# Key transposes within the second projection, a third pair of split buffers, query transposes in two parts, and compression's activation last in VectorE's queue

## The reference, cut to what matters

```
h = rms_norm(x, g_mix_norm[l]);  z = h @ w_in[l]
q, kc, vc, ks_, vs_, kw_, vw_, gl, hc, cg, bg = split(z)
q = rms_norm(q per head, g_q)                                  # 8 heads of 64
k_cmp = rms_norm(compress(kc, pe[0], w1[0], b1[0], w2[0], b2[0]), g_k[0])
v_cmp = compress(vc, pe[1], w1[1], b1[1], w2[1], b2[1])
k_slc, k_win = rms_norm(ks_, g_k[1]), rms_norm(kw_, g_k[2])
attn_out = nsa_attention(q, k_cmp, v_cmp, k_slc, vs_, k_win, vw_, gates)

def compress(k_raw, pe, w1, b1, w2, b2):     # blocks of 32 tokens, stride 16: 31 of them
    blk = blocks(k_raw) + pe
    return gelu(blk @ w1 + b1) @ w2 + b2     # w1: 2048 x 256, w2: 256 x 64
```

## Time and profile before

| | us |
|---|---|
| median of 3 runs | 1664.21 (1662.63 to 1664.91) |
| the profiled execution's own time | 1665.39 |
| its span | 1663.6 |
| TensorE busy | 1528.0 |
| GpSimd busy | 586.5 |
| VectorE busy | 764.7 |
| ScalarE busy | 455.9 |

### The profile page before, as it was taken

The page is one execution under the profiler, slowest core; times in us unless marked ns, Lnnn a source line. Parts: engine busy times, 40 slices in busy tenths (PEclk is TensorE's granted clock), DMA queues, the critical chain, the costliest instruction groups (busy, mean ns, idle before and its releaser), DMA issues.

```text
span 1663.6 us, 21240 instructions
## 1 busy us (share of the span) xinstructions
PE 1528.0 (92%) x8362; PEld 1205.2 (72%) x8362; DVE 764.7 (46%) x1461; ACT 455.9 (27%) x722; POOL 586.5 (35%) x481
## 2 busy tenths in 40 slices
PE   6978999899999999989999999999999989976885
PEld 5867787778888888867888878775588866544442
DVE  2343756549687774345513730255412254423234
ACT  4233233433131322342323332343222221100001
POOL 2473121235445444434533234421144313322222
PEclk9988999999999999989999999999999999999897
DMA  5222111034544452222322112220043589999995
GB/s 228 76 90 77 38 40 38 26 126 158 216 173 176 189 202 84 94 82 100 109 76 101 51 51 102 79 83 26 2 176 148 221 331 353 377 393 373 394 412 201
DMA packets 37348, 260.92 MB, mean 157 GB/s; under 512 B 7280, under 2 KB 7920, under 8 KB 13184
## 3 DMA queue, kind: packets, MB, share of 16 engines
q1 hardware_dynamic: 31488, 251.13, 40.0%
q0 software_dynamic: 5760, 8.41, 1.6%
HBM read 252.69 MB, written 17.30 MB: 162 GB/s over the span
## 4 chain that ended last, share of the span: by engine, by line
PE 82%; DVE 8%; issue 4%; ACT 4%; POOL 2%; DMA 1%; DVEq 0%; SPq 0%; ACTq 0%; POOLq 0%
PE G L2050 13%; PE G L2051 13%; PE G L2052 12%; PE SA L2578 4%; PE G L2578 4%; PE SA L2050 3%; PE SA L2052 3%; PE SA L2051 3%; PE PB L2052 3%; PE PB L2051 3%; PE PB L2050 3%; PE OB L2234 2%; PE G L2092 1%; PE SA L2467 1%; PE PB L2586 1%
## 5 line engine op out<-in xcount | busy, mean ns | idle before, releaser
L736 POOL TENSOR_TENSOR wl<-raw,wh 128x512 fp32r<-128x512 f32 x364 | 487.4, 1370 | 694.7 <-ACT wh L869 689.9
L869 ACT ACTIVATE wh<-raw 128x2048 fp32r<-128x2048 f32 x91 | 174.1, 1913 | 296.5 <-PE SA L2052 152.5
L2050 PE MATMUL G<-Hh,wh 128*128 128x512 f32 x544 | 218.1, 401 | 4.9 <-DVE arena L1482 1.7
L2051 PE MATMUL G<-Hl,wh 128*128 128x512 f32 x544 | 214.3, 394 | 0.0
L2052 PE MATMUL G<-Hh,wl 128*128 128x512 f32 x544 | 214.1, 394 | 0.0
L1553 DVE SCALAR_TENSOR_TENSOR arena<-arena,st 128x256 f32<-128x256 f32 x144 | 132.9, 923 | 5.1
L2050 PEld LDWEIGHTS G<-Hh,wh 128*128 128x128 f32 x544 | 103.8, 191 | 26.1 <-issue 2.3
L2052 PEld LDWEIGHTS G<-Hh,wl 128*128 128x128 f32 x544 | 103.6, 190 | 22.5
L2051 PEld LDWEIGHTS G<-Hl,wh 128*128 128x128 f32 x544 | 103.9, 191 | 20.0
L809 POOL DMA_INDIRECT raw<-xn_rows,arena x38 | 36.6, 962 | 130.4 <-PE G L2594 106.1
L2050 PE MATMUL G<-wh,Hh 128*128 128x256 f32 x256 | 77.6, 303 | 0.5 <-DVE arena L1293 0.5
(11 more groups left out here) (520 smaller groups left out, 3127.2 us busy)
## 6 DMA issues: line engine op xcount, KB each, us to landing
raw<-in_pieces_dram SPq DMA_DIRECT2D x91, 1024.0 KB, 4.8
arena<-in_pieces_dram SPq DMA_DIRECT2D x24, 1024.0 KB, 4.8
arena<-in_wexp_dram SPq DMA_DIRECT2D x11, 2048.0 KB
dn_w<-in_wexp_dram SPq DMA_DIRECT2D x18, 1024.0 KB, 42.1
arena<-in_wexp_dram SPq DMA_DIRECT2D x12, 1024.0 KB, 29.2
gu_y<-in_wexp_dram SPq DMA_DIRECT2D x6, 2048.0 KB
gu_z<-in_wexp_dram SPq DMA_DIRECT2D x5, 2048.0 KB, 45.9
gu_h<-in_wexp_dram SPq DMA_DIRECT2D x4, 2048.0 KB
```

The costliest lines, as they stand in the source:

```text
L736: ins = pool.tensor_tensor(low_[:, part], whole[:, part], high[:, part], ALU.subtract)
L869: act.activation(wh[:, split_slot(s)], wait_raw(act, sp_list[s]), ACT.Copy).then_inc(S("high_split"), 1)
L2050: pe.matmul(out, ah, bh, start=first, stop=False)
L2051: pe.matmul(out, ah, bl, start=False, stop=False)
```

## The change

TensorE takes `cT` 0 and 1 after the first half of ksvs and `cT` 2 and 3 after the second; kwvw follows. VectorE's block additions now stand ahead of the key squares, and the k squares use another part of `arena`. A third pair of split buffers, `third`, lies beneath the `alibi` table and holds piece 5 alone; the slots of later pieces alternate from there. The bias tables, whose place it shares, are therefore loaded after `cmp1` 0 is finished, behind piece 8 in SyncE's queue. The low part of piece 7 moves from GpSimd to VectorE, ahead of the copy of `cmp1` 0. The queries are normalized in two parts and transposed in two parts (heads 0 to 3 before `cmp1` 3, heads 4 to 7 after). The gelu stands after the last `queries_low`. At the start, SyncE waits for the last x tile before it issues the small weights and piece 0, and VectorE no longer waits for `con` and `par` ahead of its first statistics.

```
 def plan_groups():
...
+    g += [("kcvc", t, "a") for t in range(2)] + [("glT", 0, "a")]
+    for t in range(2):
+        g += [("ksvs", t, "a"), ("cT", 2 * t, "v"), ("cT", 2 * t + 1, "v")]
+    g += [("kwvw", t, "a") for t in range(2)]
...
-    g += [("cmp1", 2, "v"), ("cmpT", 0, "v"), ("cmp1", 3, "v"), ("cmpT", 1, "v")]
-    g += [("qT", h, "v") for h in range(NH)]
+    g += [("cmp1", 2, "v"), ("cmpT", 0, "v")]
+    g += [("qT", h, "v") for h in range(4)]
+    g += [("cmp1", 3, "v"), ("cmpT", 1, "v")]
+    g += [("qT", h, "v") for h in range(4, NH)]
...
-            early.enter_context(nc.sbuf_tensor("below_keys", [P, 12416], F32))
+            third = early.enter_context(nc.sbuf_tensor("third", [P, 2 * PIECE], F32R))
+            early.enter_context(nc.sbuf_tensor("below_keys", [P, 12416 - 2 * PIECE], F32))
...
+        VECTOR_LOWS = (7,)
+        THIRD = 5
+        def split_pair(s):
+            if s == THIRD:
+                return third[:, 0:PIECE], third[:, PIECE:2 * PIECE]
+            a = ((s + (s > THIRD)) % 2) * PIECE
+            return wh[:, a:a + PIECE], wl[:, a:a + PIECE]
+        def held_until(s):
+            return None if s == THIRD else s - 3 if THIRD < s <= THIRD + 2 else s - 2
...
             sp.dma_start(par[:, :], par_d).then_inc(S("par_loaded"), 16)
+            sp.wait_ge(S(f"tile_loaded{NT - 1}"), 16)
             sp.dma_start(smw, smw_d).then_inc(S("smw_loaded"), 16)
...
-                if n == 1:
-                    sp.wait_ge(S("sml_done"), 1)
+                if p == ("cmp", 1, 1):
+                    wait_group(sp, "cmp1", 0)
                     sp.dma_start(AR(0, BIAS["_"][1]), bias_d).then_inc(S("bias_loaded"), 16)
...
             pool.wait_ge(S("ss_k"), 1)
...
-            low(sp_list[5])
+            for p in sp_list[5:7]:
+                low(p)
             for j in range(2):
                 pool.wait_ge(S("ss_q"), j + 1)
...
-                low(sp_list[6 + j])
...
+            high(4)
+            high(5)
             for j in range(2):
-                high(4 + j)
...
+                high(6 + j)
...
-            high(6)
             for c4 in range(2):
                 keys_high(c4)
-            high(7)
+            high(8)
             for c4 in range(2, 4):
                 keys_high(c4)
-            high(8)
+            for h in range(4):
+                queries_high(h)
             high(9)
-            queries_high(0)
+            for h in range(4, NH):
+                queries_high(h)
             act.wait_ge(S("gelu_in"), 1)
...
-            dve.wait_ge(S("con_loaded"), 16)
-            dve.wait_ge(S("par_loaded"), 16)
             square_last(hraw, ss)
             norm_rows(0, hraw, rstd)
+            dve.wait_ge(S("con_loaded"), 16)
+            dve.wait_ge(S("par_loaded"), 16)
...
+            low(7)
             cmp_first(0)
             wait_freed(dve, "cmp1", 0)
             keys_low(0)
             keys_low(1)
+            queries_normed(0)
             cmp_first(1)
             keys_low(2)
             keys_low(3)
...
+            queries_normed(1)
             cmp_first(2)
             wait_freed(dve, "cmp1", 2)
             cmp_hidden(0)
+            for h in range(4):
+                queries_low(h)
             cmp_first(3)
             cmp_hidden(1)
+            for h in range(4, NH):
+                queries_low(h)
...
-            for n in ("kcvc", "ksvs", "kwvw"):
-                rows(n, (n,))
-                if n == "kcvc":
-                    narrow_turned("gl", gl_rows, 24)
-            pe.wait_ge(S("cdup_ready"), 1)
-            for c4 in range(4):
-                transposes("cT", c4, [cdup[:, t, c4].rearrange("p u d -> p (u d)") for t in range(NT)])
+            rows("kcvc", ("kcvc",))
+            narrow_turned("gl", gl_rows, 24)
+            for tp in range(2):
+                rows("ksvs", ("ksvs",), tps=(tp,))
+                pe.wait_ge(S("cdup_ready"), 1)
+                for c4 in range(2 * tp, 2 * tp + 2):
+                    transposes("cT", c4, [cdup[:, t, c4].rearrange("p u d -> p (u d)") for t in range(NT)])
+            rows("kwvw", ("kwvw",))
...
             cmp_turned(0)
+            queries_turned(0)
             cmp_first(3)
             cmp_turned(1)
+            queries_turned(1)
```

More of the change, by code:

```diff
@@ L915, in _ @@
                     free_group(ins, what, t)
+                    if s == 2 and t == 0:
+                        wait_freed(act, "cT", 3)
+                        for cc in range(2):
+                            ins = act.activation(Yh[:, 2048:4032].rearrange("p (c k g i) -> p c k g i", c=2, k=16, g=2)[:, cc],
+                                                 AR(14464, 1984).rearrange("p (c g k i) -> p c k g i", c=2, g=2, k=16)[:, cc], ACT.Copy)
+                        ins.then_inc(S("blk_high"), 1)
                 if s == 0:
@@ L1295, in _ @@
                 free_group(ins, "cT", c4)
+            wait_freed(dve, "kwvw", 1)
+            kview = Zk[:, :, 256:512]
+            ksq = AR(16512, 1024).rearrange("p (t n) -> p t n", t=NT)
+            own(dve.tensor_tensor(ksq, kview, kview, ALU.mult))
+            dve.tensor_reduce(ssqk[:, 0:16].rearrange("p (c o) -> p c o", o=1), AR(16512, 1024).rearrange("p (c d) -> p c d", d=HD), AX.X, ALU.add).then_inc(S("ss_k"), 1)
+            dve.wait_ge(S("ss_k"), 1)
+            dve.wait_ge(S("blk_high"), 1)
+            for cc in range(2):
+                ins = dve.tensor_tensor(Yl[:, 0:1984].rearrange("p (c k g i) -> p c k g i", c=2, k=16, g=2)[:, cc],
+                                        AR(14464, 1984).rearrange("p (c g k i) -> p c k g i", c=2, g=2, k=16)[:, cc],
+                                        Yh[:, 2048:4032].bitcast(F32).rearrange("p (c k g i) -> p c k g i", c=2, k=16, g=2)[:, cc], ALU.subtract)
+            ins.then_inc(S("blk_low"), 1)
             dve.wait_ge(S("rstd_k"), 1)
@@ L1342, in cmp_hidden, with queries_normed, low @@
                 free_group(ins, "cmpT", c)
-            own(dve.memset(cw[:, 864:1888], 0.0))
+            rq = rqk[:, 16:48].rearrange("p (t c) -> p t c", t=NT)
+            def queries_normed(j):
+                dve.wait_ge(S("rstd_q"), j + 1)
+                for u in range(2):
+                    ins = dve.tensor_tensor(qdup[j][:, :, :, u, :], qview[:, :, 4 * j:4 * j + 4, :],
+                                            rq[:, :, 4 * j:4 * j + 4].unsqueeze(3).to_broadcast([P, NT, 4, HD]), ALU.mult)
+                ins.then_inc(S("q_normed"), 1)
+            def low(s):
+                p = split_pieces()[s]
+                dve.wait_ge(S("high_split"), s + 1)
+                whole, (high, low_) = wait_raw(dve, p), split_pair(s)
+                high = high.bitcast(F32)
+                for q in range(4):
+                    part = slice(q * (PIECE // 4), (q + 1) * (PIECE // 4))
+                    if q == 3:
+                        dve.wait_ge(S("low_split"), s)
+                    ins = dve.tensor_tensor(low_[:, part], whole[:, part], high[:, part], ALU.subtract)
+                ins.then_inc(S("low_split"), 1)
+            low(7)
             cmp_first(0)
@@ L1371, in _ @@
             dve.tensor_scalar(hid, hid, 0.5, None, ALU.mult).then_inc(S("gelu_done"), 1)
-            for h in range(1, NH):
-                queries_low(h)
             b2k = cols(par, PAR, "b_cmp2").rearrange("p (c d) -> p c d", c=2)
@@ L2074, in wide_rows, with rows @@
                         filled(ins)
-            def rows(what, p, act=None, kts=range(KT), names=None):
+            def rows(what, p, act=None, kts=range(KT), names=None, tps=range(2)):
                 h, l = act or (Hhv, Hlv)
                 a, b = (w.rearrange("p (k n) -> p k n", n=PC) for w in weights(p))
-                for tp in range(2):
+                for tp in tps:
                     bank = group(what, names[tp] if names else tp)
```

68 lines of the change are left out of this document (19 added, 49 removed).

## The result

The changed kernel takes 1653.8 us (median of 6 runs, 1647.01 to 1654.64) beside 1664.01 us (6 runs, 1662.22 to 1665.99). The ratio is 0.9925, with a 95% interval of 0.9905 to 0.9945. The gain is 10.2 us, where 15.8 was forecast. The predicted 1648.4 is 5.4 us too low, but the range of 1642 to 1656 holds the result. The profiled execution is one of the two short ones of its six: 1647.73 us, span 1645.9.

The account below looks back on a forecast made before the run. TensorE, carrying 82% of the span, was taken as the bound, with time won where it idles or runs slower. 18.4 us at full clock less 2.6 gave 15.8, hence 1648.4 us; range 1642 to 1656.

Parts of the forecast that it names:

- Its signs: TensorE before attention: weight waits under 2 us, new copy wait about 2.6, scores at 116, first cmpk product 119 to 122.
- 1. Head: Kernel start: earlier statistics and held-back pieces gain 1.0 us; holding the pieces back does not speed x.
- 2. Transposes: Second projection: transposes moved inside it remove waits and half clock, 6.9 us; query projection ends at 88.6.
- 3. Third pair and the new wait: Compression after query projection: pieces split earlier, new copy wait to 94.8, scores at 116.4 against 136.85.
- 4. Activation last: Gelu behind the last query: wholly open, 2.4 us; cmpk at 118.8 instead of 137.19, gain 18.4 at full clock.
- 5. Clock: Compression products cmp1 1 and cmp1 3: one of the two at half clock, costing 2.6 us.
- 6. Moved parts: Bias load, pieces 9 and 10, memset: moved at no cost; bias takes 9.1 us, piece 9 low by 115 to 118.
- Rival B: Stretch 92 to 116 thinned: both products halved, head gives nothing, piece 8 late; gain 10.7, 1653.5 us; chance 0.19.
- A: Full clock in compression: no product halved; 1645.8 us, or 1641 if later half clock shifts or goes; chance 0.17.
- C: Piece 9 late behind the bias load: 5 us on the path, 1653.4 us; chance 0.04.
- D: Pieces not freed, a late load leaves the weight wait: 1661 to 1667 us; chance 0.03.
- E: Attention wholly at half clock: 20.9 us more, 1669 us, slower; chance 0.05.

Follow-up runs that it names:

- e2: The kernel before with only the two edits of the start (late small weights and pieces, statistics without table waits): 1664.46 us, ratio 0.9999.
- e5: The changed kernel with the copy of cmp1 0 ahead of the low part of piece 7 in VectorE's queue: 1648.21 us, ratio 0.9906.
- e3: The kernel before with only the transposes within the second projection and block additions ahead of the key squares: 1658.39 us, ratio 0.9964.
- e9: The changed kernel with one added wait: VectorE's key scaling starts only after GpSimd's low part of piece 5; 1653.98 us, ratio 0.9935.
- e7: The changed kernel with the gelu split around queries_low(4) and ScalarE's tanh after queries_high(4): 1653.98 us, ratio 0.9939.
- e1: The changed kernel run again, unchanged: 1652.68 us, ratio 0.9927.
- e6: e5 plus the addition of cmp1 1 ahead of the first query normalization and the second normalization behind queries_low 0 to 3: 1643.21 us, ratio 0.9879.
- e10: The kernel of e6 run again, unchanged, in more rounds: 1644.02 us, ratio 0.9883.

## Why the prediction was right, and where it was off

**The bound** and the direction were right: TensorE's waits ahead of attention were the place, and 12.3 us of the time to the first convolution product went (140.3 to 128.0). Its signs came in part: weight waits gone, a new wait for the copy. The scores started at 122.52 instead of 116.4, the first product at line 2214 at 124.87, outside the 119 to 122 that were to show it, and the clock was at 0.50 once more from 122.4 to 129.2, past the 122 that the signs of being wrong name, after 6.6 us at 1.00.

**1. Head.** `Hh` starts at 16.24 for a forecast of 16.4. x lands 7.0 us after its issue instead of 7.2 with pieces queued behind it, so holding the pieces back did not speed it here. The ring order that the Trainium skill states ("DMA: Bandwidth & Descriptors", section on queues, rings and completion order) agrees with these two rows. Of the ten traces with the pieces held back, eight show 6.7 to 7.2 us and two, e2 and e5, 6.0; what was different in those is not known. What the step gives in the total could not be measured (e2, interval of the ratio 0.999 to 1.0008).

**2. Transposes.** Right in place and size: the two waits for line 1293 are gone, the clock stays at 1.00 over the transposes, and the projection ends at 88.84 (forecast 88.6). The other nine traces of a kernel with this step have 87.29 to 89.92, so the hit to 0.2 is luck in part. Alone it gives 6.1 of the 6.9 (e3).

**3. Third pair and the new wait.** The mechanism was as forecast: weight waits gone, a new wait for the copy of `cmp1`, low part of piece 7 at 2.50 us. Its size was off: 3.94 instead of 2.6, and 7.59 us from the end of the projection to `cmp1` 1 instead of 6.2. The second wait, 3.41 us, lies in the forecast's times too (TensorE from 102.6 to the copy at 106.0), but not among its signs. The sentence that failed is "low at 82 (after rstd_k)", and with it "Piece 7 lands by 88". Two low parts stand in that chain, and I had priced both at their time alone. Piece 5's took 8.00 with VectorE's scaling of the keys beside it. Piece 4's took 6.96, because the low part of the blocks (3.89 us) now runs beside it; before, they stood apart:

```profile
67.31 4.94 POOL L736 TENSOR_TENSOR wl<-raw,wh 128x512 fp32r<-128x512 f32 x4 [6.48 <-ACT wh L869]
```

```profile
77.85 2.29 DVE L1303 TENSOR_TENSOR Yl<-arena,Yh 128x992 fp32r<-128x992 f32 x2
```

Piece 5 was low at 86.5, and SyncE issues piece 7 only then. Of the 1.6 us by which `cmp1` 1 came late this explains 0.7, the wait of VectorE for the high part. The projection ended 0.2 later, and 0.6 are the squares, 1.84 us instead of 1.23 beside the low part of piece 6. e9 shows that piece 5 is slow by its neighbour; it also shows that curing it alone gains nothing, since the slowness then falls on VectorE. I used the same slowing later for pieces 6 and 8, from the earlier trace rows, and missed it here.

**4. Activation last.** It stands open with 2.4 us, as forecast. e7 shows that the earlier place is no better in this kernel.

**5. Clock.** I allowed 2.6 us, one of two products at half. `cmp1` 1 ran wholly at half, and the transposes ahead of `cmp1` 3 and half of it too. From the forecast's 118.8 to 124.87 there are 6.1 us, read off the starts: 1.6 for the later start of `cmp1` 1; 1.6 more until `cmp1` 2 starts (102.30 against 99.1), since the half clock holds the addition up by 1.8 behind the normalization, which itself came 0.2 sooner than priced; 0.3 for the longer way from there to the next copy; 0.8 from that copy to `cmp1` 3; 1.7 for `cmp1` 3 (4.26 instead of 2.6); 0.1 behind it. From copy to `cmp1` 3 the transposes at half clock took 3.31 us, those of e5 at full clock 2.85, so 0.5 of the 0.8 are the clock's. That makes about 4.0 us for the clock, 1.4 more than the allowance, and about 2.1 for piece 7 and VectorE's queue. The term that failed is the allowance: one product at half, where both were.

**6. Moved parts.** The bias landed 12.1 us after its issue instead of 9.1, and nobody waited for it. Piece 9 was low at 120.4, against a forecast of 115 to 118, and was first needed at 128.0.

**The sum.** With a stage of 36.0 instead of 32.8 the gain would be 12.6, and the two rounds of the changed kernel show 10.2 and 11.8. In every one of the eleven traces the first product at line 2214 has come forward by more than the median: 12.3 against 10.2 here, 19.1 against 15.7 in e5, 3.6 against 0.0 in e2. So either the one trace of the kernel before is a late one, or the sentence that no later stage is tied to absolute time is not quite right; no run decides that. The profiled 17.7 holds luck in the clock's later stretches (e1). Rival B gives the right time, 1653.5, and its core is right, TensorE thinned and both products slowed. That it hits the time is luck in part, for its other items are not right: the head gave its 1.2 us on the trace, and the low part of piece 8 held nobody up. A, C, D and E did not occur: C and D would show a wait for split weights, E a clock below that before in attention, where a window of 29 us reads

```profile
122.50:151.50 29.00, 26.92 (x183) 23.92 (x184) 9.67 (x40) 9.74 (x24) 10.79 (x10) 0.85 0.18 67
```

against 0.86.

What was never asked in the prediction is whether the low part had to stand ahead of the copy. The wait of 2.6 us was written down as a price. e5 shows it was an order: 6 us of stage, 4.5 of the median. What I had derived from the Trainium skill in step 5 ("TensorE: Matmul & The Clock Gate", part 1), that the thinned stretch stays at the lower clock throughout, did not come: the clock was back at 1.00 for `cmp1` 2 in the same trace, and stayed there in e5 until 118.2, to the end of its stage, and in e6 until 112.9.

What separates the two cases is open. My own rule in step 5 went by the unbroken idle time ahead of a product, and the first trace (3.94 and 3.41 us, then half clock) and e5 (2.03 us, then full) fit it. Two other traces don't. In e1 TensorE idled 3.96 us, and the first 1.3 us of `cmp1` 1 ran at full clock:

```profile
95.12 0.30 PE L2086 MATMUL G<-wh,Yh 128*62 128x256 f32 x1 [3.96 <-DVE arena L1353]
```

```profile
95.12:96.45 1.33, 1.33 (x12) 1.33 (x12) 1.33 (x3) 0.00 (x0) 1.33 (x1) 1.00 1.27 541
```

In e3 it idled 1.88 us, less than in e5, and after 0.56 us at full clock the product ran at half (in e2, after 2.17 us, from its start):

```profile
105.84 0.33 PE L2049 MATMUL G<-wh,Yh 128*62 128x256 f32 x1 [1.88 <-POOL wl L736]
```

```profile
106.40:109.80 3.40, 3.40 (x19) 3.40 (x17) 3.40 (x3) 0.23 (x1) 3.10 (x2) 0.51 0.83 299
```

So the length of the last idle time does not tell the clock of the product behind it. What the rows do show is that the three traces of e5, e6 and e10, without the long idle times in this stretch, ran both products at full clock, and that in the four with two idle times of 3.4 us and more there (the changed kernel twice, e7, e9) both products ran at half, wholly or in part.

## What to carry to other kernels

Before pricing work that is moved onto an engine, look at what stands directly behind it in that engine's queue: a copy of 0.41 us that frees a bank belongs ahead of 2.5 us of work that only a later product reads. Price every element-wise operation of two SBUF inputs on VectorE with what GpSimd does at the same microseconds, and the other way round, at the new times and not at the old ones. And compare a stretch of the trace, from one fixed event to another, rather than one profiled total: here two executions of one kernel had stages 0.9 and 0.4 us apart, while their single totals spread over 8 us (changed kernel) and 12 us (e10).

## What the runs showed of the hardware

**VectorE and GpSimd take turns.** In e9 the scaling of the keys (2.36 us alone), the squares (1.23 alone) and the low part of piece 6 (4.95 alone) are 8.5 us of work apart; side by side they fill 83.30 to 91.30, 8.0 us. Overlap gave almost nothing. The Trainium skill ("SBUF — State Buffer", section "Who interferes with whom") says that a VectorE instruction with two SBUF inputs contends with a GpSimd instruction that reads SBUF, and calls the ports they share an exclusive lock; these rows agree. In e7 an operation with one tensor input, TENSOR_SCALAR of 128x248, went from 0.29 to 1.23 us beside GpSimd as well.

**The clock away from the change.** The same kernel had a granted clock of 0.96 or 0.74 between 720 and 760 us in two executions, and its times run from 1647.01 to 1654.7. It is one kernel in both, so the granted clock is not settled by the program alone. What decides which of the two happens was not found.
